# The first expert tables of a two-layer expert stage: three 256-column products per step in half a bank, and gelu read from the banks

## The reference, cut to what matters

```python
u = u_tab[idx]
v = v_tab[idx]
act = jax.nn.gelu(jnp.einsum('nd,nhkd->nhk', hblk, u))
return jnp.einsum('nhk,nhkd->nd', (gate * act).astype(v.dtype), v)
```

## Time and profile before

| | |
|---|---|
| Time, median of 3 runs | 2290.4 us (2287.28 to 2293.27) |
| Profiled execution, span from first to last instruction | 2285.7 us |
| The profiled execution's own time | not given apart from its span, which is 4.7 us under the median |
| PE busy | 2231.8 us (98%) |
| PEld busy | 1880.0 us (82%) |
| DVE busy | 1866.0 us (82%) |
| ACT busy | 1200.2 us (53%) |
| POOL busy | 169.6 us (7%) |
| Chain that ended last | PE 82%, DVE 10%, DMA 3%, ACT 3%, issue 2% |
| The changed sums, L2634 on DVE | 128 of 685 ns, 87.7 us |
| The changed copies, L1690 on ACT | 128 of 599 ns, 76.6 us |

### The profile page before, as it was taken

The page is one execution under the profiler, slowest core; times in us unless marked ns, Lnnn a source line. Parts: engine busy times, 40 slices in busy tenths (PEclk is TensorE's granted clock), DMA queues, the critical chain, the costliest instruction groups (busy, mean ns, idle before and its releaser), DMA issues.

```text
span 2285.7 us, 34776 instructions
## 1 busy us (share of the span) xinstructions
PE 2231.8 (98%) x13446; PEld 1880.0 (82%) x13446; DVE 1866.0 (82%) x3365; ACT 1200.2 (53%) x1754; POOL 169.6 (7%) x75
## 2 busy tenths in 40 slices
PE   8999999999999999999999999999999999999997
PEld 7788977777788888888887877788888888887886
DVE  8679996578689988888888888869998888887656
ACT  7555554456456555554444445455665554444553
POOL 0000000000044400000000000024420000000000
PEclk9999999999999999999999999999999999999999
DMA  8356593233555655555558996456555555556674
GB/s 287 129 201 215 201 350 121 86 119 104 190 173 187 189 178 172 172 175 174 170 175 306 336 352 238 147 185 192 186 184 174 171 172 175 175 171 223 215 236 132
DMA packets 123508, 442.32 MB, mean 194 GB/s; under 512 B 13760, under 2 KB 16832, under 8 KB 122704
## 3 DMA queue, kind: packets, MB, share of 16 engines
q1 hardware_dynamic: 117464, 425.04, 56.2%
q10 hardware_dynamic: 5880, 15.06, 2.0%
HBM read 436.88 MB, written 3.16 MB: 193 GB/s over the span
## 4 chain that ended last, share of the span: by engine, by line
PE 82%; DVE 10%; DMA 3%; ACT 3%; issue 2%; SPq 0%; ACTq 0%; DVEq 0%
PE psum L443 20%; PE psum L451 14%; PE psum L453 13%; PE psum L452 13%; PE psum L444 10%; PE psum L446 3%; PE psum L2865 3%; DVE low L2601 3%; PE psum L445 1%; DVE acc L1778 1%; DVE cv L2109 1%; DMA ring<-in_peer_v 1%; ACT cv L1399 1%; ACT spl L1098 1%; PE psum L919 1%
## 5 line engine op out<-in xcount | busy, mean ns | idle before, releaser
L2601 DVE TENSOR_TENSOR low<-ring,spl 128x1024 fp32r<-128x1024 f32 x638 | 779.4, 1228 | 256.1 <-ACT spl L1098 255.1
L1098 ACT ACTIVATE spl<-ring 128x1024 fp32r<-128x1024 f32 x702 | 735.1, 1053 | 281.2 <-DMA ring<-in_peer_u 157.8
L443 PE MATMUL psum<-hT,spl 128*128 128x512 f32 x2016 | 722.6, 397 | 3.0 <-DVE hT L1758 2.8
L444 PE MATMUL psum<-hT,low 128*128 128x256 f32 x2016 | 565.7, 281 | 0.0
L443 PEld LDWEIGHTS psum<-hT,spl 128*128 128x128 f32 x2016 | 380.6, 189 | 77.3 <-issue 3.4
L451 PE MATMUL psum<-spl,Ws 128*128 128x512 f32 x1024 | 411.6, 402 | 6.5 <-DVE Ws L2639 6.4
L453 PE MATMUL psum<-spl,Ws 128*128 128x512 f32 x1024 | 399.1, 390 | 0.0
L452 PE MATMUL psum<-low,Ws 128*128 128x512 f32 x1024 | 396.8, 388 | 0.0
L444 PEld LDWEIGHTS psum<-hT,low 128*128 128x128 f32 x2016 | 381.7, 189 | 9.7
L1707 ACT ACTIVATE Ws<-S 128x256 fp32r<-128x256 f32 x256 | 106.6, 417 | 361.8 <-PE psum L453 356.9
L2922 POOL TENSOR_TENSOR low<-ring,spl 128x1024 fp32r<-128x1024 f32 x64 | 163.1, 2550 | 1131.7 <-ACT spl L1098 1131.7
(11 more groups left out here) (413 smaller groups left out, 3022.2 us busy)
## 6 DMA issues: line engine op xcount, KB each, us to landing
ring<-in_peer_u SPq DMA_DIRECT2D x256, 512.0 KB, 3.5
ring<-in_peer_v SPq DMA_DIRECT2D x256, 512.0 KB, 3.6
vring<-in_ada_w SPq DMA_DIRECT2D x56, 512.0 KB, 6.0
ring<-in_w_up SPq DMA_DIRECT2D x44, 512.0 KB, 5.3
aring<-in_ada_w SPq DMA_DIRECT2D x40, 512.0 KB, 5.0
ring<-in_ab_in SPq DMA_DIRECT2D x32, 512.0 KB, 3.5
ring<-in_peer_wq SPq DMA_DIRECT2D x32, 512.0 KB, 4.3
ring<-in_w_down SPq DMA_DIRECT2D x22, 512.0 KB, 5.9
```

What stands on the lines that cost most here:

```text
L443: q.matmul(b[:, :].rearrange("p (z t) -> p z t", z=2), l[0], r, start=start, stop=False)
L444: return q.matmul(b[:, 0:256], l[1], r[:, 0], start=False, stop=False)
L1098: q.activation(P.spl[:, m % SLOTS, 0:w], P.ring[:, m % SLOTS, 0:w], ACT.Copy).then_inc(*P.hi.mark(m))
L2601: q.tensor_tensor(P.low[:, n % SLOTS, 0:w], P.ring[:, n % SLOTS, 0:w], P.spl[:, n % SLOTS, 0:w].bitcast(F32), ALU.subtract).then_inc(*P.lo ...
```

## The change

In the first table's stage `mm3_both` is replaced by `mm3` into the first half of each bank: 8 steps x 3 products of 256 columns a tile, where there were 8 x (512 + 256). The columns that TensorE streams stay at 768 a step; the products and weight loads go from 16 to 24 a tile. As all three products add up in the bank, ScalarE's copy of the second half and VectorE's sum are gone, and ScalarE's gelu reads the two banks and writes `S`. It stands where the copy stood in ScalarE's order. Waits that named the sum (`us`) now name the gelu. The query tiles keep `mm3_both`.

```diff
     for p in range(32):
         act_hi(q, P, T + 16 + 2 * p + 2)
         if p:
-            act_u2(q, P, l, p - 1)
+            act_u(q, P, l, p - 1)
         act_hi(q, P, T + 16 + 2 * p + 3)
-        if p >= 2 and p % 16 != 14:
-            for g in (p - 3, p - 2)[p % 16 != 15:]:
-                act_u(q, P, l, g)
...
     for g in range(32):
         act_hi(q, P, T + 16 + 66 + 2 * g)
-        act_u2(q, P, l, 31 + g)
-        if g == 0:
-            act_u(q, P, l, 30)
+        act_u(q, P, l, 31 + g)
         if g == 31:
             act_ws(q, P, l, 0)
             act_ws(q, P, l, 1)
         if g:
             act_hi(q, P, T + 16 + 67 + 2 * g)
-        act_u(q, P, l, 31 + g)
...
-def act_u2(q, P, l, p):
+def act_u(q, P, l, p):
...
-    q.activation(P.S[:, 2 * p:2 * p + 2, :], P.psum[:, b:b + 2, 256:512], ACT.Copy).then_inc(*act.mark(("u2", p)))
...
+    q.activation(P.S[:, 2 * p:2 * p + 2, :], P.psum[:, b:b + 2, 0:256], ACT.Gelu_apprx_tanh).then_inc(
+        *act.mark(("gelu", p)))
...
-def dve_u(q, P, l, p):
...
-    q.wait_ge(*act.at(("u2", p)))
-    q.tensor_tensor(x, P.psum[:, b:b + 2, 0:256], x, ALU.add).then_inc(*dve.mark(("us", p)))
...
     if p >= 3:
-        q.wait_ge(*dve.at(("us", p - 3)))
+        q.wait_ge(*act.at(("gelu", p - 3)))
...
         for k in range(8):
-            t = mm3_both(q, P.ps[U_BANK[p % 3] + d], cut(sl, lambda v: v[:, k * 128:(k + 1) * 128]),
-                         P.hT[:, :, k, :], k == 0, k == 7)
+            t = mm3(q, P.ps[U_BANK[p % 3] + d][:, 0:256], cut(sl, lambda v: v[:, k * 128:(k + 1) * 128]),
+                    cut(both(P.hT), lambda v: v[:, k, :]), k == 0, k == 7)
```

More of the change, by code:

```diff
@@ L368, in begin @@
         self.lo_next = 0
-        self.sum_next = [0, 0]
     def lo_at(self, n):
@@ L1010, in pe_pool @@
              lambda k, tb: (P.xr[:, tb, k * 128:(k + 1) * 128], ln_out(vact, vdve, tb, k // 4)),
-             (fold_out(P, 8), fold_out(P, 8), vdve.at(("us", 63)), vdve.at("gates1")), ("v_end",))
+             (fold_out(P, 8), fold_out(P, 8), vact.at(("gelu", 63)), vdve.at("gates1")), ("v_end",))
     for c in range(2):
@@ L1660, in act_peer @@
         if j == 0:
-            act_u2(q, P, l, 63)
             act_u(q, P, l, 63)
@@ L2612, in dve_sums @@
             dve_query(q, P, l, (n - T - 4) // 2)
-        if T + 16 <= n < T + 146:
-            while P.sum_next[l] <= (n - T - 16) // 2 - 2:
-                dve_u(q, P, l, P.sum_next[l])
 def dve_query(q, P, l, i):
@@ L2672, in dve_peer @@
         dve_lo(q, P, T + 16 + 67 + 2 * r)
-    dve_u(q, P, l, 63)
     dve_gates(q, P, 1, 0, pe, act, dve)
@@ L2877, in pe_v @@
             if j == 0:
-                q.wait_ge(*dve.at(("us", 61 + tb)))
+                q.wait_ge(*act.at(("gelu", 61 + tb)))
             t = mm3(q, P.ps[4 + 2 * tb + c][:, :], cut(both(P.Ws[:, j % 3, :, :]), lambda v: v[:, tb * 128:(tb + 1) * 128]),
```

## The result

The changed kernel takes 2297.11 us (median of 10 runs, 2294.75 to 2302.6) where the kernel before takes 2290.28 (10 runs, 2284.24 to 2293.27): ratio 1.0038, 95% interval 1.0027 to 1.0048, slower by 6 to 11 us (the medians differ by 6.8). A second comparison, with the kernel before run again beside it, gave 2298.81 against 2288.24, ratio 1.0049 (1.0032 to 1.0065). The prediction was 2303.0 and slower.

What follows compares the result with a forecast made beforehand. TensorE's product starts alone were taken to bound the first-table stages; tile and scatter-round terms gave 6.3 us a stage, 12.6 for both, added to the median 2290.4 for 2303.0 us, range 2294 to 2309.

Steps and rivals of the forecast that it cites:

- What bounds the stage: First-table stage: only the rate at which TensorE starts products sets the time; relieving VectorE and ScalarE is worth 0.
- The first 30 tiles: Start of each first-table stage: tile period goes from 2.777 to 2.827 us, +1.5 us a stage.
- The next 34 tiles: First-table tiles after the first transposes: period goes from 2.793 to 2.827 us, +1.2 us a stage.
- The rounds beside the scatter: 32 rounds of scatter and two tiles: 6.23 against 6.12 us, with 0.10 for the restart; +3.6 us a stage.
- A: Main forecast: first-table products start at the up projection's rate, +12.6 us for both stages; chance 0.70.
- B: First-table stage: TensorE's time goes by columns alone, so no change, 2290 or 2294 us with restarts; chance 0.14.
- B's milder form: First-table steps: the added product has a fixed cost of 0.003 us, 6 us in all, 2296 us.
- the prediction's own line for slower: Whole-kernel total: above 2297.3 us counts as slower, from a no-change bound of 0.3%, 6.9 us.
- D: First-table stage: new sequence falls into a slower pace throughout, 4.4 us on top, 2307.4 us; chance 0.10.
- C: First-table steps: second product with the same weights needn't wait for a load, -9 us, 2281 us; chance 0.06.
- Covers: First-table stage: bank gelu of 0.60 to 0.62 us comes two blocks, 11 us, before TensorE needs it; cost 0.
- the signs: Marks of being right in the profile: among them VectorE's busy time down 88 us, ScalarE's about 77, no time following.

Runs made afterwards that it cites:

- The relief alone: Changed kernel with the old wide and narrow products, gelu reading the banks' first half, no copy or sum; ratio 0.9996 to the kernel before.
- TensorE's part: Kernel before, copies and sums kept, wide product split into two of 256 columns in the inner 6 of 8 steps; ratio 1.0057, median 2299.67 us.
- the other order: Changed kernel with a step's three products ordered high x high, low x high, high x low; stage 380.75 us, one run 2301.09 us.
- two bank pairs: Changed kernel with two pairs of banks instead of three, TensorE waiting for the gelu of two blocks earlier; one run 2297.14 us.

## Why the prediction was right, and where its size was off

- **What bounds the stage** held: TensorE's starts alone. The relief alone was worth nothing, the product split alone made the kernel slower.
- **The first 30 tiles**, predicted +1.5 us: the part from the last score product to the transposes went from 83.42 to 84.94, +1.52. The choice of the same instruction sequence in the up projection, and not of neighbouring narrow products, was the right one: 0.353 a step there and here.
- **The next 34 tiles**, predicted +1.2: +1.1 against the first trace of before (95.63 to 96.77 from there to the scatter), +1.7 against the first layer of its second trace. The old pace after the transposes isn't fixed, which one trace couldn't tell.
- **The rounds beside the scatter**, predicted +3.6, are the first term that was mis-sized: +3.2 (195.84 to 199.04). The round is 6.22 and not 6.23 us: the restart adds 0.08 as it did before, where 0.10 was taken from a restart after a wait.
- **The sum**: 5.9 us a layer and 11.7 in all, where 12.6 was predicted.
- **The total** was predicted as 2290.4 + 12.6 = 2303.0 and came out at 2297.1 and 2298.8. In the second comparison the base accounts for it, a median of three runs: the 23 runs of the kernel before have 2288.24, and 2288.2 + 11.7 = 2299.9 is a little above the result. In the first it doesn't: all ten runs of the kernel before have 2290.28, and 2290.3 + 11.7 = 2302.0 is 4.9 us over the result. That remainder lies outside the two stages. There the two traces of the kernel before have 1535.9 and 1536.1 us (span less both stages), the two of the changed kernel 1535.5 and 1534.8, and the four runs with the relief, TensorE's part, the other order and two bank pairs 1532.0 to 1538.3. So the two kernels differ less there than runs that change nothing outside the stages differ among themselves; that the first total came out low by chance is likely, not shown.
- **What was luck**: the first total alone would not have told A from B. At 2297.1 it is nearer to B's milder form (2296) than to 2303.0, and it lies 0.2 us under the prediction's own line for slower (2297.3). "Slower" holds by the ratio's interval and by the second comparison, and A's mechanism by the stage lengths. The chances don't quite add up either: A and D are 0.80, where slower has 0.82, and C alone is 0.06, where faster has 0.05.
- **Covers**: gelu from the banks takes 0.60 us, as bounded; TensorE never waited for it, not even with one block less of cover. The busy times fell by 81 and 67 us, not by the 88 and about 77 of the signs: the durations of all instructions together fell by 89 and 78, but the page counts time in which two of an engine's instructions overlap only once. VectorE's waits for ScalarE's high parts grew instead (352.6 us of idle time ahead of its low parts, where the kernel before has 255.1): the freed time became idle time.
- **Rivals**: B's milder form had the sign and the mechanism of a fixed cost for the added product, but half its size: the traces have 353.3 - 347.1 = 6.2 ns a step. The rule of the Trainium skill named there (TensorE: Matmul & The Clock Gate, Back-to-back issue gap), which that section gives for products by themselves and not for a stream with loads, has 2.5 ns of it; the measurement decides. B's starting point, a narrow product at just half the wide one's 0.230, was a rounding: over the first tiles of the trace before, the gaps after a narrow product average 0.1163, and in a row of narrow ones they are 0.1178. C is refuted by the other order. D didn't come about: the new sequence had one pace in both stretches.

## What to carry to other kernels

Where TensorE's starts are the whole chain, count products as well as columns: splitting a 512-column product in two costs some 6 ns here at the same number of columns (some 9 in a mixture with unsplit ones), and two thousand of them are more than 11 us. Time taken off engines that nothing waits for comes back as their idle time, however much it is (148 us here). A price is best taken from the same instruction sequence elsewhere in the trace: that gave 0.353 us a step, while counting products alone gave 4.2 of the mixture's 6.7 us. For a change of 0.5%, compare the length of the stage and not totals alone: those of the unchanged kernel lay between 2284 and 2295 us, which is as much.

## What the runs showed of the hardware

- In a run of products, each with its own load of 128 columns of weights, the starts are 0.110 to 0.113 us apart, with 128 or with 192 columns; only the first one behind wider products holds the next off for less (0.09 us with 192). At 256 they start 0.118 apart, at 384 0.173 to 0.178, at 512 0.228 to 0.230 on average. The Trainium skill (TensorE: Matmul & The Clock Gate, LDWEIGHTS (loading the stationary operand)) gives a load in ns as its columns over 1.2, an estimated 107 ns for 128. The 0.11 us agree with it, though each load's row is 0.19 us long: the rows overlap.
- A change from 16-bit products of 64 columns to the wide or narrow 32-bit ones holds the second of them off for 0.08 us, and doing it half as often gains 0.10 each time.
- One instruction sequence can have two paces that differ by 0.6%, each kept over some 30 tiles (2.777 and 2.793 us in the earlier trace rows), and which one it has can change from one execution to the next: the first layer's second stretch had 2.793 in one trace of the kernel before and the faster pace in the other. The cause is open.
